# Attention stage: one fused instruction for scale, mask and row maximum; normalisation moved from probabilities to outputs; PSUM copies shared between two engines

## What is computed

```python
def _sink_softmax(scores, sink):
    snk = sink[:, :, None]
    m = snk
    for s in scores:
        m = jnp.maximum(m, jnp.max(s, axis=-1))
    ex = [jnp.exp(s - m[..., None]) for s in scores]
    denom = jnp.exp(snk - m)
    for e in ex:
        denom = denom + jnp.sum(e, axis=-1)
    return [e / denom[..., None] for e in ex]
...
    q, k = rope(q), rope(k)
    s_win = jnp.where(valid[None, :, None, None], s_win, -jnp.inf)
    p_win, p_ctx = _sink_softmax([s_win, s_ctx], snk)
    o = (jnp.einsum('bnhgqk,bnkhd->bnqhgd', p_win.astype(v.dtype), vw)
         + jnp.einsum('bnhgqk,bkhd->bnqhgd', p_ctx.astype(vc.dtype), vc))
    y = o.reshape(B, L, D_MODEL) @ w_out
```

## Time and profile before

| what | us |
|---|---|
| median of 3 runs | 2007.94 |
| lowest and highest run | 2002.89 and 2009.8 |
| span of the profiled execution, which is also taken as its own time | 2005.2 |
| first DVE instruction of attention unit 0 | at 1690.43 |
| first matmul of `ato` | at 1772.92 |

### The profile page before, as it was taken

One profiled execution on the slowest core, in us unless ns is written; L12 is line 12 of the kernel. 1 busy time (PEld: TensorE's weight loads), 2 busy tenths in 40 slices (PEclk: granted clock), 3 DMA queues, 4 the chain that ended last, 5 costly groups with the idle time before them and its releaser, 6 DMA issues.

```text
span 2005.2 us, 34209 instructions
## 1 busy us (share of the span) xinstructions
PE 1843.1 (92%) x14608; PEld 1577.2 (79%) x14608; DVE 942.6 (47%) x1675; ACT 770.8 (38%) x1330; POOL 461.2 (23%) x226
## 2 busy tenths in 40 slices
PE   5998999888899999998899889999999988789999
PEld 3787897877789997886787567888888776479998
DVE  1658525566443334535776544222222247944333
ACT  3453522333355455332532234222222344645443
POOL 0135212121034342211230011121212111013443
PEclk7998998989899999999998889999999989999999
DMA  8443343222465445222120113323322337025553
GB/s 313 163 159 128 117 150 132 86 107 86 156 248 188 173 173 182 84 89 91 63 85 1 64 66 145 126 105 126 108 103 100 131 119 270 1 95 192 179 187 127
DMA packets 36582, 261.59 MB, mean 130 GB/s; under 512 B 4048, under 2 KB 4176, under 8 KB 6224
## 3 DMA queue, kind: packets, MB, share of 16 engines
q1 hardware_dynamic: 36432, 259.40, 35.5%
HBM read 258.34 MB, written 1.05 MB: 129 GB/s over the span
## 4 chain that ended last, share of the span: by engine, by line
PE 76%; DVE 13%; ACT 4%; issue 4%; DMA 2%; POOL 1%; SPq 0%; DVEq 0%; ACTq 0%
PE ps L815 18%; PE ps L816 18%; PE ps L817 18%; PE ps L866 2%; PE ps L842 2%; PE ps L832 1%; POOL wl L733 1%; DVE msq L2402 1%; PE ps L1084 1%; PE ps L833 1%; PE ps L834 1%; PE ps L1072 1%; PE ps L874 1%; ACT wh L1447 1%; DVE sc L2595 1%
## 5 line engine op out<-in xcount | busy, mean ns | idle before, releaser
L733 POOL TENSOR_TENSOR wl<-raw,wh 128x1024 fp32r<-128x1024 f32 (+1 forms) x179 | 426.2, 2383 | 1332.7 <-ACT wh L1447 1332.7
L815 PE MATMUL ps<-h_hi,wh 128*128 128x256 f32 (+1 forms) x1696 | 556.0, 328 | 7.3 <-POOL wl L733 5.1
L816 PE MATMUL ps<-h_lo,wh 128*128 128x256 f32 (+1 forms) x1696 | 547.9, 323 | 0.0
L817 PE MATMUL ps<-h_hi,wl 128*128 128x256 f32 (+1 forms) x1696 | 547.6, 323 | 0.0
L1447 ACT ACTIVATE wh<-raw 128x1024 fp32r<-128x1024 f32 (+1 forms) x330 | 342.2, 1040 | 403.3 <-PE ps L817 291.2
L815 PEld LDWEIGHTS ps<-h_hi,wh 128*128 128x128 f32 x1696 | 326.4, 192 | 37.1 <-POOL wl L733 9.7
L816 PEld LDWEIGHTS ps<-h_lo,wh 128*128 128x128 f32 x1696 | 326.4, 192 | 25.7 <-issue 2.4
L817 PEld LDWEIGHTS ps<-h_hi,wl 128*128 128x128 f32 x1696 | 326.2, 192 | 23.8
L1947 DVE TENSOR_TENSOR wl<-raw,wh 128x1024 fp32r<-128x1024 f32 (+1 forms) x151 | 187.5, 1242 | 242.6 <-ACT wh L1447 231.5
L815 PE MATMUL ps<-gh,wh 128*128 128x256 f32 (+1 forms) x528 | 169.2, 321 | 0.0
L816 PE MATMUL ps<-gl,wh 128*128 128x256 f32 (+1 forms) x528 | 168.1, 318 | 0.0
(11 more groups left out here) (409 smaller groups left out, 2777.3 us busy)
## 6 DMA issues: line engine op xcount, KB each, us to landing
raw<-in_mod SPq DMA_DIRECT2D x72, 1024.0 KB, 4.9
raw<-in_ffn_in SPq DMA_DIRECT2D x66, 1024.0 KB, 4.8
raw<-in_ffn_out SPq DMA_DIRECT2D x24, 1024.0 KB, 4.8
raw<-in_w_in SPq DMA_DIRECT2D x16, 1024.0 KB, 4.8
raw<-in_w_gate SPq DMA_DIRECT2D x12, 1024.0 KB, 4.9
raw<-in_w_ab SPq DMA_DIRECT2D x12, 1024.0 KB, 4.8
raw<-in_ffn_out SPq DMA_DIRECT2D x12, 768.0 KB, 4.2
raw<-in_w_at SPq DMA_DIRECT2D x5, 1024.0 KB, 5.0
```

Of the source, the lines that this page charges most:

```text
L733: nc.gpsimd.tensor_tensor(wl[e % SPLIT][:, 0:entries[e]["words"]], part(e), wh[e % SPLIT][:, 0:entries[e]["words"]].bitcast(F32), ALU.subt ...
L815: nc.tensor.matmul(b[:, cols], wh[e % SPLIT][:, w], xh(k), start=(k == 0), stop=False)
L816: nc.tensor.matmul(b[:, cols], wh[e % SPLIT][:, w], xl(k), start=False, stop=False)
L817: ins = nc.tensor.matmul(b[:, cols], wl[e % SPLIT][:, w], xh(k), start=False, stop=(k == nk - 1))
```

## The change

A unit's instructions become these:

- The queries' norm weight `qnw` and the sinks are negated once (`nqnw`, `nsink`), and the mask is +BIG, so all scores are negated. One `tensor_tensor_reduce` per half (line 2611 of the new file) adds the mask, multiplies by `rq` and takes the minimum, starting from the negated sink. Lines 2599 and 2601 go; line 2602's place is taken by one subtraction of the sinks (2616).
- ACT waits for the fused instruction itself and takes the exponentials with scale -1; the two sink exponentials become one of 128 x 2 (1928).
- PE transposes the exponentials as they are, and waits for ACT (`e_ready`) instead of DVE. DVE's multiplication of 128 x 1024 goes.
- DVE's reciprocals (`r_ready`) are turned into a row per head and spread over the 64 rows of that head by two matmuls with the identity (1423), into a new PSUM tile `rs`; ACT copies it to `rinv` (1935). DVE multiplies the output tile by it into `otmp` (2641). `aoh` and `aol` are made from `otmp`.
- ACT copies the first `pt` tile, DVE the second (2635).
- `ato`'s first tile waits for `aol` block by block.

The diff:

```diff
@@ -379,6 +379,7 @@
         if 1 <= u <= 16:
             add("pt", u - 1, 0)
             add("pt", u - 1, 1)
+            add("rs", u - 1)
         if u >= 2:
             add("ao", u - 2)
     use([("ato", 0), ("ato", 1)])
@@ -554,6 +555,10 @@
     artmp = sb("artmp", [P, 2, L], arena + 21504)
     rq = sb("rq", [P, KD, 4], tiny_at + 64)
     tin4 = sb("tin4", [P, 3, 16], tiny_at)
+    nsink = tiny[:, 128:144]
+    nqnw = tiny[:, 144:145]
+    rinv = sb("rinv", [P, 2, P], arena + 19456)
+    otmp = sb("otmp", [P, 2, P], arena + 19456 + 2 * P)
 
     def K2(name):
         a, b = C2[name]
@@ -1404,17 +1409,24 @@
             if u == 0:
                 mod(3)
             if 1 <= u <= 16:
-                pe.wait_ge(sem("p_ready"), u)
+                pe.wait_ge(sem("e_ready"), u)
                 for hf in range(2):
                     b = begin("pt", u - 1, hf)
                     for c in range(NC):
                         ins = nc.tensor.transpose(b[:, P * c:P * c + P], sc3[:, (u - 1) % 3, hf, P * c:P * c + P],
                                                   ident)
                     close(ins)
+                pe.wait_ge(sem("r_ready"), u)
+                b = begin("rs", u - 1)
+                for hf, h in enumerate(HALF):
+                    by = tin4[:, (u - 1) % 3, 4 + hf:5 + hf].to_broadcast([P, 64])
+                    ins = nc.tensor.matmul(b[h, 0:P], by, ident, start=True, stop=True)
+                close(ins)
             if u >= 2:
                 w_ = u - 2
                 if u == 2:
                     evacuated(pe, "av", 0, NC - 1)
+                evacuated(pe, "pt", w_, 0)
                 evacuated(pe, "pt", w_, 1)
                 b = begin("ao", w_)
                 for c in range(NC):
@@ -1423,9 +1435,8 @@
                                                start=(c == 0), stop=(c == NC - 1))
                 close(ins)
         for m in range(KD):
-            if m == 0:
-                evacuated(pe, "ao", 15)
-            dense(("ato", m), lambda k: aoh[:, k, :], lambda k: aol[:, k, :], KD, slice(0, L))
+            dense(("ato", m), lambda k: aoh[:, k, :], lambda k: aol[:, k, :], KD, slice(0, L),
+                  (lambda k: pe.wait_ge(sem("ao_lo"), 2 * k + 2)) if m == 0 else None)
             behind("c2", m, sqh2)
         ffn("2", "c2", 1)
 
@@ -1892,13 +1903,14 @@
             full(act, "aqss", i)
             free(A(rq[:, i, :], bank("aqss", i)[:, 0:4], ACT.Sqrt, bias=S("eps64"), scale=64.0), "aqss", i)
 
+        act.wait_ge(sem("neg_ready"), 1)
         for i in range(8):
             ahead("aq", i)
             full(act, "aq", i)
             if i >= 2:
                 query_root(i - 2)
             A(asq[:, i % 2, 0:L], bank("aq", i)[:, 0:L], ACT.Square).then_inc(sem("q_sq"), 1)
-            free(A(aq[:, i, :], bank("aq", i)[:, 0:L], ACT.Copy, scale=S("qnw")), "aq", i)
+            free(A(aq[:, i, :], bank("aq", i)[:, 0:L], ACT.Copy, scale=nqnw), "aq", i)
             if i >= 2:
                 mod()
         for i in (6, 7):
@@ -1907,23 +1919,24 @@
             if u == 1:
                 mod(3)
             if u < 16:
+                t4 = tin4[:, u % 3, :]
+                evacuated(act, "as", u, 1)
+                for hf in range(2):
+                    A(sc3[:, u % 3, hf, :], sc3[:, u % 3, hf, :], ACT.Exp, bias=t4[:, 2 + hf:3 + hf], scale=-1.0,
+                      accum_out=t4[:, 4 + hf:5 + hf])
                 act.wait_ge(sem("s_ready"), u + 1)
-                t4 = tin4[:, u % 3, :]
-                for hf in range(2):
-                    A(sc3[:, u % 3, hf, :], sc3[:, u % 3, hf, :], ACT.Exp, bias=t4[:, 2 + hf:3 + hf],
-                      accum_out=t4[:, 4 + hf:5 + hf])
-                    ins = A(t4[:, 6 + hf:7 + hf], S("sink")[:, 2 * (u // 2) + hf:2 * (u // 2) + hf + 1], ACT.Exp,
-                            bias=t4[:, 2 + hf:3 + hf])
-                ins.then_inc(sem("e_ready"), 1)
+                A(t4[:, 6:8], t4[:, 8:10], ACT.Exp).then_inc(sem("e_ready"), 1)
             if 1 <= u <= 16:
                 w_ = u - 1
-                for hf in range(2):
-                    full(act, "pt", w_, hf)
-                    free(A(PTa[:, w_ % 2, hf], bank("pt", w_, hf).rearrange("p (c q) -> p c q", c=NC), ACT.Copy),
-                         "pt", w_, hf)
+                full(act, "pt", w_, 0)
+                free(A(PTa[:, w_ % 2, 0], bank("pt", w_, 0).rearrange("p (c q) -> p c q", c=NC), ACT.Copy),
+                     "pt", w_, 0)
+                full(act, "rs", w_)
+                free(A(rinv[:, w_ % 2, :], bank("rs", w_)[:, 0:P], ACT.Copy), "rs", w_)
             if u >= 2:
-                full(act, "ao", u - 2)
-                A(aoh[:, (u - 2) // 2, P * (u % 2):P * (u % 2) + P], bank("ao", u - 2)[:, 0:P],
+                w_ = u - 2
+                evacuated(act, "ao", w_)
+                A(aoh[:, w_ // 2, P * (w_ % 2):P * (w_ % 2) + P], otmp[:, w_ % 2, :],
                   ACT.Copy).then_inc(sem("ao_hi"), 1)
         for m in range(KD):
             ahead("ato", m, depth=min(SPLIT, KD + 2 - m))
@@ -2567,6 +2580,8 @@
             evacuated(dve, *sw)
             return V.tensor_tensor(x, x, t, ALU.add)
 
+        V.tensor_scalar(nsink, S("sink"), -1.0, None, ALU.mult)
+        V.tensor_scalar(nqnw, S("qnw"), -1.0, None, ALU.mult).then_inc(sem("neg_ready"), 1)
         for key in [("ak", 0), ("ak", 1)] + [("av", 0, c) for c in range(NC)] + [("aq", 0)]:
             ahead(*key)
         for z in range(2):
@@ -2587,19 +2602,19 @@
         for u in range(16 + 3):
             if u < 16:
                 if u >= 3:
-                    full(dve, "pt", u - 3, 1)
+                    full(dve, "rs", u - 3)
+                i = u // 2
                 t4 = tin4[:, u % 3, :]
                 for hf in range(2):
                     full(dve, "as", u, hf)
-                    by = rq[:, u // 2, 2 * (u % 2) + hf:2 * (u % 2) + hf + 1]
-                    free(V.scalar_tensor_tensor(sc3[:, u % 3, hf, :], bank("as", u, hf), by,
-                                                window[:, 512 * (u % 2):512 * (u % 2) + 512],
-                                                ALU.mult, ALU.add), "as", u, hf)
+                    by = rq[:, i, 2 * (u % 2) + hf:2 * (u % 2) + hf + 1]
+                    free(V.tensor_tensor_reduce(sc3[:, u % 3, hf, :], bank("as", u, hf),
+                                                window[:, 512 * (u % 2):512 * (u % 2) + 512], by,
+                                                nsink[:, 2 * i + hf:2 * i + hf + 1], ALU.add, ALU.min,
+                                                t4[:, 2 + hf:3 + hf]), "as", u, hf)
                 evacuated(dve, "as", u, 1)
-                link(V.tensor_reduce(t4[:, 0:2], sc3[:, u % 3], AX.X, ALU.max))
-                i = u // 2
-                link(V.tensor_tensor(t4[:, 0:2], t4[:, 0:2], S("sink")[:, 2 * i:2 * i + 2], ALU.max))
-                V.tensor_scalar(t4[:, 2:4], t4[:, 0:2], -1.0, None, ALU.mult).then_inc(sem("s_ready"), 1)
+                V.tensor_tensor(t4[:, 8:10], t4[:, 2:4], nsink[:, 2 * i:2 * i + 2],
+                                ALU.subtract).then_inc(sem("s_ready"), 1)
             if u == 1:
                 mod(3)
             if 1 <= u <= 16:
@@ -2607,15 +2622,24 @@
                 t4 = tin4[:, w_ % 3, :]
                 dve.wait_ge(sem("e_ready"), w_ + 1)
                 link(V.tensor_tensor(t4[:, 4:6], t4[:, 4:6], t4[:, 6:8], ALU.add))
-                link(V.reciprocal(t4[:, 4:6], t4[:, 4:6]))
-                V.tensor_tensor(sc3[:, w_ % 3], sc3[:, w_ % 3], t4[:, 4:6].unsqueeze(2).to_broadcast([P, 2, T]),
-                                ALU.mult).then_inc(sem("p_ready"), 1)
+                V.reciprocal(t4[:, 4:6], t4[:, 4:6]).then_inc(sem("r_ready"), 1)
             if u >= 3:
                 w_ = u - 3
                 dve.wait_ge(sem("ao_hi"), w_ + 1)
                 o = slice(P * (w_ % 2), P * (w_ % 2) + P)
-                free(V.tensor_tensor(aol[:, w_ // 2, o], bank("ao", w_)[:, 0:P], aoh[:, w_ // 2, o].bitcast(F32),
-                                     ALU.subtract), "ao", w_)
+                V.tensor_tensor(aol[:, w_ // 2, o], otmp[:, w_ % 2, :], aoh[:, w_ // 2, o].bitcast(F32),
+                                ALU.subtract).then_inc(sem("ao_lo"), 1)
+            if 1 <= u <= 16:
+                w_ = u - 1
+                full(dve, "pt", w_, 1)
+                free(V.tensor_copy(PTa[:, w_ % 2, 1], bank("pt", w_, 1).rearrange("p (c q) -> p c q", c=NC)),
+                     "pt", w_, 1)
+            if 2 <= u <= 17:
+                w_ = u - 2
+                full(dve, "ao", w_)
+                evacuated(dve, "rs", w_)
+                free(V.tensor_tensor(otmp[:, w_ % 2, :], bank("ao", w_)[:, 0:P], rinv[:, w_ % 2, :], ALU.mult),
+                     "ao", w_)
         project("ato", 2, (LT,))
         inverse("c2")
         norm("c2", 5, (LT,))
@@ -2694,7 +2718,7 @@
```

(2 more changed lines are left out.)

## The result

The changed kernel takes 1984.8 us (median of 4 runs, 1981.02 to 1989.93) against 2006.93 (4 runs). The ratio is 0.9895, with a 95% interval of 0.987 to 0.9919: 22 us, or 1.1%, faster. On a second chip it took 1987.2 us (6 runs) against 2006.94, ratio 0.9909 (0.9888 to 0.993). The forecast was 1996.9 us with a range of 1989.5 to 2004.0: right in direction, with half of the gain, and outside its range.

A forecast was written before the change was run, and what follows sets the result against it. DVE's list bounds the attention loop; after the change a 4.08 us cycle through DVE and PE does. `ato` starts at 1705.7 + 49.0 + 7.2 = 1761.9, 11.0 us earlier: 2007.94 - 11.0 = 1996.9 us, range 1989.5 to 2004.

The forecast's parts named there:

- The bound: Attention loop: DVE's list is the period, 4.69 us a unit; what follows the loop is paced by PE.
- The ring: Attention loop: fused pair, transposes, spreading, output matmuls and `otmp` form a cycle through DVE and PE, 4.08 us a unit.
- p: Fused pair on DVE, first start to end of second accumulator read: taken as 1.70 us, between 1.40 and 2.66.
- issue gap: PE's pause before the next matmul group: 0.17 us, counted after the transposes and again after the spreading.
- The start: Units 0 to 3: unit 3 at 1705.7 us, middle of 1705.0 to 1706.4, against 1704.38 before; 1.3 us lost.
- unit 2 no earlier than now: Loop start: unit 2 waits for the first transposes and starts at 1700.9 us, later than in the kernel before.
- The end: Unit 15's start to `ato`'s first matmul: 7.2 us instead of 11.93.
- the forecast's own rule: Whole loop: gain is 11.0 - 15 x (p - 1.70) us, so 15.5 at 1.40 and zero at 2.43.
- The slow fused instruction: Rival, DVE scores: fused instruction streams at half rate, p 2.80, 5.18 us a unit, kernel 2013.4 us; chance 0.05.
- The fourth rival: Loop: issue gaps hide behind waits, PE's 3.3 to 3.4 or DVE's 3.44 us is the period, 1989 us; chance 0.04.
- Longer handovers: Rival, loop: six steps between engines cost 0.4 us more a unit, 5.2 us in all, 2002.1 us; chance 0.12.
- Half clock: Rival, loop: PE stays at half clock, 5.48 us a unit, kernel 7.8 us slower at 2015.7; chance 0.03.

The follow-up runs named there:

- the two extra instructions: Changed kernel plus one DVE sum per unit, result unused, either in DVE's wait or ahead of the fused pair: period 3.75 and 4.09 us.
- e3_copies_on_act: Changed kernel with both `pt` tiles copied by ACT and DVE's copy removed: period 3.75 us, loop 63.59 us.
- the second profile: The changed kernel itself profiled once more, with no edit: period 3.75 us, loop 66.30 us.
- e9_scores_late: Changed kernel with PE's order per iteration made transposes, output matmuls, scores, spreading: 1982.88 us, ratio 0.9884, period 3.48 us.

## Why the prediction was right or wrong

**The bound** The earlier trace rows was right: DVE's list was the period of the loop, PE the bound behind it, and what the loop gave back reached the end (232.3 us from `ato` on, in both).

**The ring** was right in its members and their order, shown by the two extra instructions: 0 in the wait, 0.34 on the ring for an instruction of 0.41. Its sum was too large, 4.08 instead of 3.75. The terms, from the unit above:

| step of the ring | predicted | measured |
|---|---|---|
| start of the fused pair to the second transposes on PE | 1.75 | 1.59 |
| these transposes, to the spreading | 0.60 | 0.59 |
| spreading, to the output's first weight load | 0.38 | 0.16 |
| output matmuls, to `otmp` | 1.15 | 1.20 |
| `otmp`, to the next pair | 0.20 | 0.21 |

Two terms failed. The read of the accumulator was taken as 0.15 on top of 0.70; in fact it runs beside the next instruction, and the step from one fused instruction to the next is 0.73. The second read ends with the second instruction (1726.65), so p, from the first start to the end of the second read, was 1.54 and not 1.70. The whole second instruction is longer (806 ns against 741), but not one read is added to the sum. And the issue gap of 0.17, read between long groups, was put behind the spreading too, where there is none; 0.22 of the term is that gap and a shorter spreading. The two make 0.38 of a unit, and the other three terms give 0.05 back: 12 x 0.33 = 4.0 us over twelve units.

**The sentence on the Trainium skill's "The DRAIN you can't avoid"** (VectorE: DVE Perf Modes) would have moved p up, to 1.82. The trace went the other way: a step of 0.73 for an instruction of 0.806, whose read of 0.084 starts together with the next instruction. The same section of the Trainium skill adds that a next operation that is not held starts earlier, which the forecast did not take up and with which this step agrees.

**The start** was predicted as 15.3 us from unit 0 to unit 3, as the middle of full and half clock. It was 12.02 at a clock of 0.99 and 14.83 at 0.77. The mechanism, that unit 2 now waits for the first transposes, holds: unit 2 came 8.39 us after unit 0 at full clock and 10.45 at half, where the forecast had 10.5. Without DVE's copy (`e3_copies_on_act`) it came after 6.74 at full clock. The step that failed is that half clock was carried over from the kernel before; the forecast let full clock come only after unit 2 and gave it 0.7 us. This was worth 3.3 us in the first profile and 0.4 in the second. The sign "unit 2 no earlier than now" failed in the first profile (8.39 against 9.44 before) and held in the second. Why the clock fell in one execution and not in the other no run here shows.

**The end** was predicted as 7.2 us and was 6.44. The last transposes start 3.30 us after unit 15, not 3.75, which is 0.45 of the miss; the spreading without its gap is 0.22 again, and the last output matmuls are 0.09 shorter.

The misses of the first profile add up: 3.25 + 3.96 + 0.76 = 7.97 us over the forecast's 11.0 gives the loop's 19.0. The further 3.1 us of the medians are not explained by the loop. p was 1.54, between its lower bound of 1.40 and the 1.70 taken, and by the forecast's own rule that is worth only 2.4 us. The range ended too early at 1989.5 because it let p vary and hardly the gaps or the clock in the start.

**The rivals.** The slow fused instruction did not occur, and the note of the Trainium skill on halved throughput (Vector Engine (DVE) Microarchitecture Reference, "Points that are easy to get wrong") had no part in it: 32 instructions with one source in PSUM took 801 to 811 ns. Whether the rule holds with both sources in SBUF no run here shows. The fourth rival, a shorter ring, came nearest, in half its size: one of the two gaps was absent, but the ring stayed the period. Longer handovers did not occur: the forecast's sum has two between engines and two issue gaps, not the six steps that the rival counted, and the two handovers took 0.05 us each (1726.65 to 1726.70, 1728.60 to 1728.65). Half clock reached the first units of the second profile and none of the twelve after them.

**What the prediction did not ask** is what each part is worth. It had the numbers for that. It read the ring of 4.08 as a limit to the gain. By its own terms the fused instruction alone, with the multiplication kept, has a list of 1.70 + 0.16 + 0.17 + 1.22 + 0.28 = 3.53 us and no ring through PE, which is less than 4.08; measured were 3.23 and 3.75. So they said that the second part costs more than it saves.

## What to carry to other kernels

Taking work off the busiest engine does not help if what replaces it makes that engine wait for another within the same unit. Add up both the list of each engine and each ring through several engines, for each part of a change alone; here the fused instruction gave 23.1 us of loop, and the rest took 4 us of it back, though its waiting block by block gains 0.8 to 1.2 by itself. An instruction on the list costs its start-to-start step, not its length, and a difference of a few microseconds ahead of the changed place should be subtracted before the change is credited with it.

## What was not expected of the hardware

- An instruction that masks, scales and takes the minimum of 128 x 512 out of PSUM takes 806 ns with a step of 0.73 us to the next; before, a half of a unit took a step of 0.66 us for the scores and half of the 1.22 us of the reduction for the same. The read of its result, 84 ns, lies within the next one.
- The changed kernel had 0.3 and 6.8 us of half clock in the first units of the loop in its two profiled executions, and took 12.02 and 14.83 us for units 0 to 2. Over the thirteen profiles, whose programs hardly differ up to there, unit 0 started between 1683.1 and 1695.1.
- A unit's score matmuls of 64 x 512, in both halves of the array, hold PE for 1.06 us at full clock before the next group's weight load (`e9_scores_late`).
